# Skip weights folded into a scan's kernels, and the input turns of the scan moved in front of the first attention logits

## The chip, the cores and the metric

The program runs on one core of a Trainium2 chip. A core has a matrix engine (PE, with its weight loads PEld), a vector engine (VectorE, DVE in the rows), a scalar engine (ScalarE, ACT), GpSimd (POOL) and SyncE (SP), which here only issues DMAs. The metric is the device time of one execution in microseconds (us), the median of several runs. Matrix sums go to PSUM banks of 512 fp32 columns, which VectorE and ScalarE empty.

## The reference, cut to what matters

The program is a chain of transformer blocks; only one branch of the first and its neighbour are touched. `u` is 512 columns of the first projection, in 32 groups of 16 channels:

```python
uf = u.reshape(bsz, L, SSM_GROUPS, SSM_GROUP)           # 1024 tokens, 32 groups of 16
bu = einsum('gnp,blgp->blgn', B, uf)                    # complex, 64 states a group
s  = associative_scan(decay, bu)
y  = (einsum('gpn,blgn->blgp', C_re, s_r) - einsum('gpn,blgn->blgp', C_im, s_i)
      + D_skip.reshape(SSM_GROUPS, SSM_GROUP) * uf)
y  = gelu(y.reshape(bsz, L, SSM_WIDTH))
y  = y * sigmoid(y @ w_glu + b_glu)
```

Beside it stands sparse attention: for each of 8 heads and 8 blocks of 128 queries, logits against the keys up to the block, a mask of the 256 best keys (found earlier), softmax, and the product with the values. `D_skip` is the skip weight: each channel's input is added to its output, times one number.

## The kernel before, in words

Three stages matter, one after the other, each ended by all engines.

**`first_projection`** computes the projection. SP issues its loads and stores; between the second weight load and the first store it issues 12 small loads of gains (`HeadRows.load_gains`, L537).

**`sparse_prepare`** (about 180 to 215 us) turns queries and keys and, in between, makes the scan's weights. In `scan_group`, PE makes for every odd group four *kernels* of the scan: `K` (16 input channels by 128 = 8 time steps times 16 output channels) is the sum of two products of 64 states (L2026). `K` goes to memory and comes back later as a block of a Toeplitz matrix. There are eight such groups of four. Per block of 128 rows PE does eight turns (L2039), four turns of other weights (L2021), and the eight products of a `K` group. VectorE scales the next block's rows (L1993) before PE can turn them.

**`attend_and_scan`** (about 431 to 688 us) does attention and the scan together. Attention is a list of 64 *items*: pair of heads `n // 16`, block `n % 16 // 2`, head `n % 2`. Each item is: `logits(n)` on PE (L2600), `mask(n)` on VectorE (L2718), `exps(n)` on ScalarE (L2885), `turn(n)` on PE (L2610), `move(n)` on ScalarE (L2892), and every second item `values` on PE (L2619). `logits` runs two items ahead. Each engine's order is written out by one loop over `n`; the scan is threaded into it by the table `place`, which says at which item, and at which of two spots in it, a group of the scan's work is issued. The groups are eight each of:

- TURN_U: PE turns the regrouped inputs (L2628); ScalarE moves them to SBUF (L2915). Item 0 to 3.
- SUM_IN: PE multiplies them with the input weights (L2640); ScalarE moves (L2919). Items 4 to 7. After the last, VectorE and GpSimd run the scan itself in steps, one an item, from item 8 (`SCAN_AT`): L2738 on for VectorE, L2529 on for GpSimd.
- SUM_OUT: PE adds kernel part and state part (L2659, L2660); VectorE adds them to the inputs that were multiplied with the skip weights (L2804). Items 30 to 33, 35 and 36.
- Gelu on ScalarE at item 36 (L2953), then TURN_Y (L2667, moved in L2923), items 37 to 40, and MIX (L2678, L2930), items 41 to 48.

The skip multiplications are eight VectorE instructions of 128x512 (L2853), one an item at items 4 to 11. They wait only for GpSimd's regrouping (L2513).

Before the first logits the keys and the first queries are split in an upper and a lower part, in two halves of the columns: `upper_half` on ScalarE (L2876, L2869, L2871), `lower_half` on VectorE (L2822, L2825). The first half comes first of all, the second at item 0; it is needed for `logits(8)`. The TURN_U groups use three PSUM banks in turn, two of which are the second banks of the logits, which items 0 to 7 of a pair do not need.

## Time and profile before

| | us |
|---|---|
| median of three runs | 3916.5 |
| the three runs | 3909.71, 3976.51, 3916.5 |
| the profiled execution | 3910.52 |
| its span | 3908.8 |
| `sparse_prepare` in it | 180 to 215 |
| `attend_and_scan` in it | 431 to 688 |

The span is what the profiler saw of the instructions; the execution's own time has 1.7 us more around it. Times in rows count from the start of the span. PE is busy for 94% of the span, but that mean is over many stages; the two stages above are to be read from their own windows.

### The profile page before, as it was taken

To read this page: it belongs to the slowest core of one execution; us is meant where nothing else is said; L and a number is where in the kernel's file an instruction comes from. 1 tells how busy PE (TensorE), PEld (TensorE's weight loads), DVE (VectorE), ACT (ScalarE), POOL (GpSimd) and SP (SyncE) were. 2 spreads that over 40 slices of the span, in tenths; PEclk is the share of its full clock that TensorE was granted. 3 is DMA by queue.
4 is the path that set the end of the run, shared out by engine and by line. 5 is a ranking of instruction groups with operands and counts; after the bars stand their busy time and mean duration, and the time that the engine had idled before them with its cause. 6 is when DMAs were issued, how large, how long until landed. Compare 5 with 4: busy or idle time off the path is not lost. (4 is left out here: it accounts for less than half of the span.)

```text
span 3908.8 us, 53307 instructions
## 1 busy us (share of the span) xinstructions
PE 3665.5 (94%) x19688; PEld 3115.3 (80%) x19688; DVE 2537.2 (65%) x4296; ACT 1819.5 (47%) x3398; POOL 1219.0 (31%) x1199
## 2 busy tenths in 40 slices
PE   7999789898999999999999978899999999999898
PEld 6868666777888788788878877778899999999876
DVE  6679664346777576312675578876567777776666
ACT  3256466135333345321444457755445555545444
POOL 1423320141111101111235451100566666666400
PEclk9989999999999999999999989999999999999999
DMA  4322221562676574521235587855211111111064
GB/s 153 113 81 92 92 50 68 183 211 88 207 256 231 196 273 138 162 103 49 79 122 180 172 184 140 168 199 167 53 33 53 46 39 44 55 39 44 22 243 140
DMA packets 348750, 485.37 MB, mean 124 GB/s; under 512 B 45435, under 2 KB 219036, under 8 KB 344636
## 3 DMA queue, kind: packets, MB, share of 16 engines
q1 hardware_dynamic: 311580, 371.33, 30.2%
q0 software_dynamic: 34608, 106.45, 9.4%
q10 hardware_dynamic: 2304, 4.20, 0.3%
q8 instruction: 157, 2.57, 0.3%
q14 instruction: 101, 0.83, 0.1%
HBM read 337.43 MB, written 144.47 MB: 123 GB/s over the span
## 5 line engine op out<-in xcount | busy, mean ns | idle before, releaser
L119 PE MATMUL banks<-l_first_ws,l_XT 128*128 128x256 f32 x2880 | 359.6, 284 | 0.0
L119 PEld LDWEIGHTS banks<-l_first_ws,l_XT 128*128 128x128 f32 x2880 | 348.8, 192 | 0.0
L119 PE MATMUL banks<-l_XT,hg_ws 128*128 128x512 f32 x1440 | 343.2, 394 | 0.0
L119 PEld LDWEIGHTS banks<-l_XT,hg_ws 128*128 128x128 f32 x1440 | 266.7, 189 | 52.5
L4898 POOL TENSOR_TENSOR hg_DD<-hg_BB 128x256 f32<-128x256 f32 x224 | 173.9, 776 | 259.3 <-PE banks L4651 133.4
L4751 DVE TENSOR_TENSOR hg_DD<-hg_Q,hg_DD 128x256 f32<-128x256 f32 x224 | 204.7, 914 | 73.3 <-ACT hg_DD L4824 73.2
L119 PE MATMUL even_bank<-l_first_ws,l_XT 128*128 128x512 f32 x888 | 207.8, 392 | 3.2 <-PEq L909 1.9
L119 PE MATMUL even_bank<-even_ws,l_XT 128*128 128x512 f32 x876 | 204.4, 390 | 0.0
L119 PEld LDWEIGHTS even_bank<-l_first_ws,l_XT 128*128 128x128 f32 x888 | 167.3, 189 | 41.2 <-issue 6.0
L119 PEld LDWEIGHTS even_bank<-even_ws,l_XT 128*128 128x128 f32 x876 | 163.9, 188 | 34.0
L119 PE MATMUL am_g_acc<-l_XT,am_ws 128*128 128x512 f32 x768 | 176.1, 391 | 0.0
L4899 POOL TENSOR_TENSOR hg_DD<-hg_BB 128x256 f32<-128x256 f32 x224 | 170.2, 760 | 0.0
L119 PEld LDWEIGHTS am_g_acc<-l_XT,am_ws 128*128 128x128 f32 x768 | 144.2, 188 | 32.2 <-issue 0.8
L119 PE MATMUL down_acc<-down_first_split 128*128 128x512 f32 x696 | 162.7, 392 | 3.3 <-PEq L1496 3.3
L4751 DVE TENSOR_TENSOR hg_DD<-hg_KK,hg_DD 128x256 f32<-128x256 f32 x224 | 165.3, 738 | 0.0
L119 PEld LDWEIGHTS down_acc<-down_first_split 128*128 128x128 f32 x696 | 131.8, 189 | 31.2 <-issue 3.7
L4866 ACT ACTIVATE hg_junk<-banks 128x128 f32<-128x128 f32 x128 | 35.3, 276 | 227.1 <-DVE hg_O L4768 227.1
L4651 PE MATMUL banks<-hg_DD 128*128 128x128 f32 x896 | 121.8, 280 | 12.9 <-DVE hg_AT L4705 10.3
L3285 ACT ACTIVATE even_stage<-even_bank 128x512 f32<-128x512 f32 x48 | 28.7, 598 | 219.7 <-PE even_bank L119 219.7
L4651 PEld LDWEIGHTS banks<-hg_DD 128*128 128x128 f32 x896 | 115.8, 196 | 17.3 <-issue 6.9
L4824 ACT ACTIVATE hg_DD<-hg_DD 128x1024 f32<-128x1024 f32 x112 | 118.3, 1056 | 14.3 <-POOL hg_DD L4899 13.8
L119 PE MATMUL banks<-l_XT 128*128 128x512 f32 x504 | 121.0, 399 | 2.5 <-PEq L4562 1.9
(771 smaller groups left out, 9213.8 us busy)
## 6 DMA issues: line engine op xcount, KB each, us to landing
l_first_raw<-in_odd_w_in SPq DMA_DIRECT2D x64, 512.0 KB, 5.5
l_first_raw<-in_even_w_in SPq DMA_DIRECT2D x16, 1024.0 KB, 5.4
l_room_tiles<-hidden SPq DMA_DIRECT2D x63, 256.0 KB, 6.9
da_first_X<-q_k_hi POOLq DMA_DIRECT2D x24, 512.0 KB, 8.0
da_first_X<-q_k_lo POOLq DMA_DIRECT2D x24, 512.0 KB, 13.1
l_room_tiles<-y_even SPq DMA_DIRECT2D x45, 256.0 KB, 5.7
ffn_y<-in_w_ffn_down SPq DMA_DIRECT2D x22, 512.0 KB, 4.5
weight_sums_w_ffn_down<-ffn_y SPq DMA_DIRECT2D x11, 1024.0 KB, 4.2
```

Source lines behind the costliest of these rows:

```text
L119: mm = pe.matmul(out, lhs(p, k), rhs(q, k), start=start and i == 0, stop=stop and i == n - 1, skip_group_check=skip)
L3285: act.activation(stage[:, i % B, :], bank[:, i % B, :], chunks[i // G][2]).then_inc(moved, 1)
L4651: mm = pe.matmul(pA[:, u % 2, i * P:(i + 1) * P], DD[:, buf(n, l), 0, i, :], DD[:, buf(n, l), 1, i, :], start=True, stop=True, skip_group_ ...
L4751: last = dve.tensor_tensor(d, sides(x[:, s, :], h)[:, :, e, :, u, :], d, ALU.mult)
L4824: act.activation(d, d, ACT.Exp).then_inc(es, 1)
L4866: act.activation(junk[:, j % 2, :], pO[:, j % 2, 0:R_D], ACT.Square, accum_out=hs[:, sb, 0, j:j + 1]).then_inc(sqd, 1)
L4898: pool.tensor_tensor(factors(n, j, 1)[:, :, :, 1 - e, :], b[:, :, :, 1 - e, :], mid, ALU.subtract)
L4899: last = pool.tensor_tensor(factors(n, j, 0)[:, :, :, e, :], mid, b[:, :, :, e, :], ALU.subtract)
```

## The change

Four things are changed, all in the stages above.

1. The skip weights go into the kernels `K`. They are loaded early, as 16 x 32 numbers; VectorE makes from them 32 diagonal blocks of 16 x 16 (`through`), and in `scan_group` PE adds one to the first 16 columns of each kernel, by a product with the identity between the two that were there. The eight skip multiplications are gone, the later addition of outputs to inputs becomes a copy, and the skip load in front of the stage too.
2. TURN_U 0 to 2 are issued in front of the first logits, 3 to 6 at item 0, 7 at item 1. VectorE moves them, not ScalarE.
3. The second half of keys and queries is split at item 3, not 0. The exp table is loaded after the first casts, not before.
4. All later scan work is issued earlier: SUM_IN by one item, the scan's steps by one, SUM_OUT and all behind it by two. SUM_IN 4 and 5 and TURN_Y 3 and 4 use other banks.

```diff
@@ HeadRows
+        self.skip_w = place.sb("skip", [S_CH, S_GROUPS], side="right")
     def load_gains(self, sp):
+        sp.dma_start(self.skip_w[:, :], self.skip.rearrange("(g q) -> q g", q=S_CH),
+                     allow_slow_non_contiguous=True).then_inc(self.skip_ld, DMA)
         sp.wait_ge(self.ones, 1)
@@ sparse_prepare, VectorE, then PE
+                dve.wait_ge(head.skip_ld, DMA)
+                dve.tensor_tensor(through[:, :, :], ident[0:S_CH, 0:S_CH].unsqueeze(1).to_broadcast([S_CH, S_GROUPS, S_CH]),
+                                  head.skip_w[:, :].unsqueeze(2).to_broadcast([S_CH, S_GROUPS, S_CH]), ALU.mult).then_inc(diagonal, 1)
                 mean_of(0)
...
+                    if i == 1:
+                        pe.wait_ge(diagonal, 1)
...
-                        for c in range(2):
-                            mm = pe.matmul(acc[0:S_CH, b, q * P:(q + 1) * P], ss.cB[rows, c, j, :], ss.CP[rows, c, j, 0:S_T, :],
-                                           start=c == 0, stop=c == 1)
+                        pe.matmul(out, ss.cB[rows, 0, j, :], ss.CP[rows, 0, j, 0:S_T, :], start=True, stop=False)
+                        pe.matmul(out[:, 0:S_CH], ident[0:S_CH, 0:S_CH], through[:, 2 * j + n % 2, :], start=False, stop=False,
+                                  skip_group_check=True)
+                        mm = pe.matmul(out, ss.cB[rows, 1, j, :], ss.CP[rows, 1, j, 0:S_T, :], start=False, stop=True)
@@ attend_and_scan, the table of places
-        place[k // 2, k % 2] = TURN_U + k
-        place[4 + k // 2, k % 2] = SUM_IN + k
-        place[(30 + k, 1) if k < 4 else (35 + (k - 4) // 2, k % 2)] = SUM_OUT + k
-        place[37 + k // 2, k % 2] = TURN_Y + k
-        place[41 + k, 1] = MIX + k
+        place.setdefault(((-1, 0), (-1, 0), (-1, 0), (0, 0), (0, 0), (0, 1), (0, 1), (1, 0))[k], []).append(TURN_U + k)
+        place[3 + k // 2, k % 2] = [SUM_IN + k]
+        place[(28 + k, 1) if k < 4 else (33 + (k - 4) // 2, k % 2)] = [SUM_OUT + k]
+        place[35 + k // 2, k % 2] = [TURN_Y + k]
+        place[39 + k, 1] = [MIX + k]
-    bank_no.update({SUM_IN + k: (8 + k) % 3 if k < 4 else 0 for k in range(8)})
+    bank_no.update({SUM_IN + k: (8 + k) % 3 if k < 6 else 0 for k in range(8)})
-    bank_no.update({TURN_Y + k: (1, 2, 0, 0, 0, 0, 0, 0)[k] for k in range(8)})
+    bank_no.update({TURN_Y + k: (1, 2, 0, 1, 2, 0, 0, 0)[k] for k in range(8)})
-    SKIP_AT, HALVE_AT, SCAN_AT, GELU_AT, MULT_AT = 4, 10, 8, 36, 49
+    LATER_AT, HALVE_AT, SCAN_AT, GELU_AT, MULT_AT = 3, 10, 7, 34, 47
@@ VectorE
-                    dve.tensor_tensor(yv, bank_at(SUM_OUT + k).rearrange("c g (s q) -> c g s q", q=S_CH), yv, ALU.add).then_inc(out_add, 1)
+                    dve.tensor_copy(yv, bank_at(SUM_OUT + k).rearrange("c g (s q) -> c g s q", q=S_CH)).then_inc(out_add, 1)
+                        if TURN_U <= g < SUM_IN:
+                            k = g - TURN_U
+                            dve.wait_ge(u_made, k + 1)
+                            dve.tensor_copy(U[:, 4 * k:4 * k + 4, :], bank_at(g)).then_inc(u_moved, 1)
-                    if n == 0:
+                    if n == LATER_AT:
                         lower_half(1)
-                    if SKIP_AT <= n < SKIP_AT + S_T:
-                        s = n - SKIP_AT
...
-                        dve.tensor_tensor(uc[:, s, :], uc[:, s, :], skip_w, ALU.mult).then_inc(skipped, 1)
@@ ScalarE
+                upper_half(0)
                 act.preload_act_table_set(LOG_EXP)
-                upper_half(0)
-                    if n == 0:
+                    if n == LATER_AT:
                         upper_half(1)
```

VectorE's order at the start of `attend_and_scan`, before. L2822 and L2825 are the lower parts of keys and queries; L2718 (ISA) is a mask, with its row minimum as a row of its own.

```order
L2822 TENSOR_TENSOR aa_K<-merge_first_F,aa_K 128x512
L2825 TENSOR_TENSOR aa_X<-merge_first_F,aa_X 64x512 x2
L2718 ISA aa_S,aa_least<-aa_pS,att_M 128x128
L2718 ISA aa_least 128x1
L2718 ISA aa_S,aa_least<-aa_pS,att_M 128x128
L2718 ISA aa_least 128x1
L2822 TENSOR_TENSOR aa_K<-merge_first_F,aa_K 128x512
L2825 TENSOR_TENSOR aa_X<-merge_first_F,aa_X 64x512 x2
L2718 ISA aa_S,aa_least<-aa_pS,att_M 128x256
```

The same place now. L2832 is VectorE's move of a TURN_U group (line numbers differ between the kernels).

```order
L2832 COPY aa_three<-aa_acc 128x512
L2832 COPY aa_three<-aa_pS 128x512 x2
L2839 TENSOR_TENSOR aa_K<-merge_first_F,aa_K 128x512
L2842 TENSOR_TENSOR aa_X<-merge_first_F,aa_X 64x512 x2
L2731 ISA aa_S,aa_least<-aa_pS,att_M 128x128
L2731 ISA aa_least 128x1
L2731 ISA aa_S,aa_least<-aa_pS,att_M 128x128
L2731 ISA aa_least 128x1
L2832 COPY aa_three<-aa_acc 128x512
L2832 COPY aa_three<-aa_pS 128x512 x2
L2832 COPY aa_three<-aa_acc 128x512
L2731 ISA aa_S,aa_least<-aa_pS,att_M 128x256
```

Three copies now stand ahead of the first split, and four between the second mask and the third, where the second split stood.

ScalarE's order at items 3 and 4 now. L2897 is an exp, L2904 a move of turned exps, L2930 a move of a SUM_IN group, L2914 and L2915 empty a bank of values, L2888 to L2883 are the upper parts of the second half.

```order
L2897 ACTIVATE aa_E<-aa_S,aa_least 128x384
L2930 ACTIVATE aa_three<-aa_pS 128x4x128
L2904 ACTIVATE aa_ET<-aa_pE 128x2x128
L2914 ACTIVATE aa_part<-aa_pO 64x128
L2915 ACTIVATE aa_yo<-aa_pO 64x128
L2914 ACTIVATE aa_part<-aa_pO 64x128
L2915 ACTIVATE aa_yo<-aa_pO 64x128
L2930 ACTIVATE aa_three<-aa_acc 128x4x128
L2888 ACTIVATE aa_K<-merge_first_F 128x512
L2881 ACTIVATE aa_X<-merge_first_F 64x512
L2883 ACTIVATE aa_X<-merge_first_F 64x512 x2
L2897 ACTIVATE aa_E<-aa_S,aa_least 128x384
```

The second half's casts now stand between the exps of items 4 and 5, behind two SUM_IN moves and the first emptying of values; before, they stood at item 0, behind two TURN_U moves.

## Rows read from the trace of the kernel before

**Rows 1.** The page: the span, and busy time of each engine with its share.

```profile
span 3908.8 us, 53307 instructions
PE 3665.5 (94%) x19688; PEld 3115.3 (80%) x19688; DVE 2537.2 (65%) x4296; ACT 1819.5 (47%) x3398; POOL 1219.0 (31%) x1199
```

**Rows 2.** Windows: stretch, length; busy of PE, PEld, DVE, ACT, POOL; clock; DMA share, GB/s.

```profile
437.00:453.00 16.00, 11.97 (x54) 10.51 (x54) 6.28 (x19) 10.87 (x25) 0.45 (x1) 0.69 0.76 199
453.00:470.00 17.00, 16.69 (x173) 13.40 (x174) 5.02 (x13) 12.24 (x28) 0.04 (x1) 1.00 0.01 2
470.00:500.00 30.00, 19.55 (x90) 16.11 (x89) 29.65 (x32) 16.55 (x30) 19.67 (x10) 0.83 0.02 9
500.00:530.00 30.00, 24.18 (x118) 18.69 (x117) 28.76 (x37) 19.56 (x50) 11.82 (x5) 0.94 0.03 10
575.00:600.00 25.00, 17.01 (x88) 14.52 (x89) 7.52 (x16) 21.49 (x34) 0.00 (x0) 0.80 0.12 42
```

**Rows 3.** Timeline, 431 to 446: start, busy, engine, line, operation, [idle before <- releaser].

```profile
431.08 1.28 ACT L2933 ACT_TABLE_LOAD   x1 [0.57 <-PEq L2132]
431.26 4.44 POOL L2513 COPY aa_three<-att_scan_inputs 128x1024 f32<-128x1024 f32 x4 [7.04 <-POOLq L2132]
434.83 2.13 DVE L2825 TENSOR_TENSOR aa_X<-merge_first_F,aa_X 64x512 fp32r<-64x512 f32 x2 [1.01 <-ACT aa_X L2871]
437.11 1.85 PE L2600 MATMUL aa_pS<-aa_K,aa_X 128*128 128x128 f32 x6 [8.16 <-DVE aa_X L2825]
438.75 1.06 PE L2628 MATMUL aa_acc<-ident,aa_three 128*128 128x128 f32 x4
439.85 0.60 ACT L2915 ACTIVATE aa_three<-aa_acc 128x512 f32<-128x512 f32 x1 [0.88 <-PE aa_acc L2628]
445.78 0.62 PE L2600 MATMUL aa_pS<-aa_K,aa_X 128*128 128x384 f32 x2 [2.56 <-DVE aa_least L2718]
```

**Rows 4.** Timeline, 453 to 472: the SUM_IN groups and the scan's first step.

```profile
456.39 1.09 PE L2640 MATMUL aa_pS<-aa_three 128*64 128x128 f32 x16
464.42 0.82 DVE L2718 CUSTOM_DVE_ANT_0 aa_S<-aa_pS,att_M 128x640 f32<-128x640 f32 x1 [2.21 <-PE aa_pS L2600]
465.33 1.56 PE L2619 MATMUL aa_pO<-aa_ET,att_V 128*128 128x256 f32 x6
469.77 1.23 DVE L2738 TENSOR_TENSOR merge_first_F<-aa_three,aa_s_wide 128x1024 f32<-128x1024 f32 x1 [3.71 <-ACT aa_three L2919]
```

**Rows 5.** The skip multiplications: all eight by line, then the timeline, 471 to 487.

```profile
L2853 DVE TENSOR_TENSOR att_scan_inputs<-att_scan_inputs,merge_first_F x8: 684/687/2844, 449.7 to 489.1; 128x512 f32<-128x512 f32 x8
...
471.79 2.00 DVE L2853 TENSOR_TENSOR att_scan_inputs<-att_scan_inputs,merge_first_F 128x512 f32<-128x512 f32 x1
479.38 2.36 POOL L2535 TENSOR_TENSOR merge_first_F<-aa_three,aa_s_wide 128x1024 f32<-128x1024 f32 x1
479.45 2.84 DVE L2853 TENSOR_TENSOR att_scan_inputs<-att_scan_inputs,merge_first_F 128x512 f32<-128x512 f32 x1
482.32 4.51 DVE L2830 TENSOR_TENSOR aa_X<-merge_first_F,aa_X 64x1024 fp32r<-64x1024 f32 x2
```

**Rows 6.** DMA issues, 530 to 566 us: line, count, KB each, us to landing.

```profile
aa_s_wide<-scan_out SPq DMA_DIRECT2D x8, 256.0 KB, 5.4
```

**Rows 7.** Timeline, 577 to 583: PE waits for a bank behind ScalarE's Gelu work.

```profile
581.74 1.51 PE L2600 MATMUL aa_pS<-aa_K,aa_X 128*128 128x512 f32 x4 [4.45 <-ACT aa_three L2923]
```

**Rows 8.** Timeline, one period of `sparse_prepare`, then the nearest small products.

```profile
194.13 1.64 PEld L2026 LDWEIGHTS ap_acc<-l0s_s_wide,l0s_s_cB 64*16 64x16 f32 x16 [0.17 <-issue]
195.98 0.86 PEld L2039 LDWEIGHTS ap_pT<-ident,ap_xs 128*128 128x128 f32 x8 [0.21 <-DVE ap_xs L1993]
...
1654.33 0.66 PE L3155 MATMUL even_bank<-ident,even_t 16*128 16x16 f32 x8
```

**Rows 9.** SP's timeline, 39 to 48: the gains' loads, and the first store.

```profile
39.13 5.09 SPq L537 DMA_DIRECT2D l0s_gc<-in_q_norm_g  x8
47.75 11.56 SPq L604 DMA_DIRECT2D first_projection<-l0s_stage  x3
```

More of the change, by code:

```diff
@@ L517, with __init__ @@
     EARLY, WIDTH = 4, 964
-    def __init__(self, place, gains):
-        self.gains, self.place = gains, place
+    def __init__(self, place, gains, skip):
+        self.gains, self.place, self.skip = gains, place, skip
         self.raw = place.sb("first_raw", [P, KD, NC], side="right")
@@ L523, in __init__ @@
         self.gain = place.sb("gc", [P, 8], side="right")
+        self.skip_w = place.sb("skip", [S_CH, S_GROUPS], side="right")
+        self.skip_ld = place.sem("skip_loaded")
         flat = self.raw[:, :, :].rearrange("p k n -> p (k n)")
@@ L1871, in sparse_prepare @@
         stage = pl.sb("stage", [P, B, NC])
+        through = pl.sb("through", [S_CH, S_GROUPS, S_CH])
         pT = pl.ps("pT", [P, 2, 8, P])
@@ L2341, in __init__ @@
         self.uc = self.room[:, :].rearrange("c (s f) -> c s f", s=S_T)
-        self.skip, self.m8, self.bias = F[:, 7, 0:S_W], F[:, 7, S_W:S_W + S_J], F[:, 7, S_W + S_J:S_W + S_J + 4]
-        self.uc_ld, self.m8_ld, self.skip_ld, self.bias_ld = (
-            place.sem(n) for n in ("inputs_loaded", "radius_loaded", "skip_loaded", "mix_bias_loaded"))
+        self.m8, self.bias = F[:, 7, 0:S_J], F[:, 7, S_J:S_J + 4]
+        self.uc_ld, self.m8_ld, self.bias_ld = (place.sem(n) for n in ("inputs_loaded", "radius_loaded", "mix_bias_loaded"))
         self.loads = [(self.uc, p1[:, 0:S_W].rearrange("(c s) f -> c s f", s=S_T), self.uc_ld),
                       (self.m8, kept["m8"], self.m8_ld),
-                      (self.skip, prm["D_skip"].partition_broadcast(P), self.skip_ld),
                       (self.bias, prm["b_glu"].rearrange("(k p) -> p k", p=P), self.bias_ld)]
@@ L2407, in attend_and_scan @@
         t1, t2, p1t, p2t, p3t = (F[:, r, :].rearrange("p (j c) -> p j c", c=S_C) for r in (5, 6, 4, 0, 1))
-        skip_w, m8, bias = begun.skip, begun.m8, begun.bias
-        uc_ld, m8_ld, skip_ld, bias_ld = begun.uc_ld, begun.m8_ld, begun.skip_ld, begun.bias_ld
+        m8, bias, uc_ld, m8_ld, bias_ld = begun.m8, begun.bias, begun.uc_ld, begun.m8_ld, begun.bias_ld
         sum_banks = [acc[:, :, :]] + [pS[:, a, 1, :].rearrange("p (q n) -> p q n", n=P) for a in range(2)]
@@ L2682, in scan_part, with scan_group @@
                 def scan_part(n, spot):
-                    g = place.get((n, spot), -1)
+                    for g in place.get((n, spot), ()):
+                        scan_group(g)
+                def scan_group(g):
                     if TURN_U <= g < SUM_IN:
@@ L2693, in scan_part @@
                         mix_outputs(g - MIX)
+                scan_part(-1, 0)
                 pe.wait_ge(k_split, 1)
@@ L2814, in scan_part @@
                 def scan_part(n, spot):
-                    g = place.get((n, spot), -1)
-                    if SUM_OUT <= g < TURN_Y:
-                        add_output(g - SUM_OUT)
+                    for g in place.get((n, spot), ()):
+                        if TURN_U <= g < SUM_IN:
+                            k = g - TURN_U
+                            dve.wait_ge(u_made, k + 1)
+                            dve.tensor_copy(U[:, 4 * k:4 * k + 4, :], bank_at(g)).then_inc(u_moved, 1)
+                        elif SUM_OUT <= g < TURN_Y:
+                            add_output(g - SUM_OUT)
                 def lower_half(half):
@@ L2833, in _ @@
                 steps = scan_states()
+                scan_part(-1, 0)
                 lower_half(0)
@@ L2910, in scan_part, with scan_group @@
                 def scan_part(n, spot):
-                    g = place.get((n, spot), -1)
-                    if TURN_U <= g < SUM_IN:
-                        k = g - TURN_U
-                        act.wait_ge(u_made, k + 1)
-                        act.activation(U[:, 4 * k:4 * k + 4, :], bank_at(g), ACT.Copy).then_inc(u_moved, 1)
-                    elif SUM_IN <= g < SUM_OUT:
+                    for g in place.get((n, spot), ()):
+                        scan_group(g)
+                def scan_group(g):
+                    if SUM_IN <= g < SUM_OUT:
                         k = g - SUM_IN
@@ L4966, in build_program @@
             late = Place(nc, "l0s").__enter__()
-            head = HeadRows(late, (a["q_norm_g"][0], a["k_norm_g"][0], a["idx_k_norm_g"][0]))
+            head = HeadRows(late, (a["q_norm_g"][0], a["k_norm_g"][0], a["idx_k_norm_g"][0]), a["D_skip"][0])
             with Place(nc, "l0w") as pw:
```

10 lines of the change are left out of this document (4 added, 6 removed).

## The prediction

> **What bounds the kernel now.** The page's shares [rows 1] say that PE is busy for 94% of the span, but the change touches two stages of some 290 us, so I read windows of them first [rows 2], then the timeline where PE has gaps. In `attend_and_scan` the bound changes place. From 437 to 453 PE is busy for 11.97 of 16 us at a granted clock of 0.69, a mixture of both levels (1.2 and 2.4 GHz); it then runs full until the last SUM_IN group (16.69 of 17 us at 1.00). From 470 to 500 VectorE is the bound (29.65 of 30 us, PE 19.55), and still from 500 to 530 (28.76, PE 24.18): attention's masks stand in one queue with the scan's steps. From 575 to 600 it is ScalarE (21.49 of 25, PE 17.01), with Gelu and the moves behind it. Outside these, PE is. A microsecond taken from VectorE is worth one only between 470 and about 535.
>
> The start, by its timeline [rows 3]: ScalarE loads a table for 1.28 us, casts, and VectorE splits; the first logits start at 437.11, 8.16 us after PE's last work. TURN_U groups follow, 1.06 us for four turns at the low level, each moved by ScalarE in 0.60. The splits of the second half hold VectorE, and PE waits 2.56 us for a mask. The scan's first step starts at 469.77, 3.71 us after VectorE's last work [rows 4], waiting for the last SUM_IN move.
>
> **The change, part by part.** Sums are made against the profiled execution's own time, 3910.5 us.
>
> *The start.* The table load no longer precedes the casts: 1.28 us earlier. In front of the first split VectorE now copies three groups. Regrouping takes GpSimd 4.44 / 4 = 1.11 us a quarter [rows 3], so its second quarter, which the third group needs, is there at 433.5. Three groups of turns behind it end at about 435 (one of 1.06 us after 433.5, plus a second's rest), the copy at 435.7. A copy of this shape out of PSUM isn't in the rows on VectorE; ScalarE's takes 0.60, an element-wise one on VectorE 0.69 [rows 5]; I take 0.65. Then the splits (0.1 to 0.8 us for the keys and 2.13 for the queries; with GpSimd's copies over, some 2.3 together): first logits at 438.0, **0.9 us later**, with three groups done.
>
> *From there to the scan's first step.* PE was busy for 11.97 + 16.69 = 28.7 us from 437 to 470 [rows 2]. Off go three groups of 1.06 (3.2) and one item's attention work, since SUM_IN ends at item 6: the values there alone are 1.56 us [rows 4], with a logits and a turn I take 3. That leaves 22.5. Onto it come new waits, which follow from the order. The mask of item 5 stands behind the second split, and that behind ScalarE's queue of item 3: two SUM_IN moves (1.2), the emptying of a bank (about 1.1, four short instructions), the casts (2.5, the distance from the table load's end to the first query split in [rows 3]), then 2.1 for the split. That is 7 us of standstill on VectorE, with only some 5 us of PE work ready in it (four SUM_IN groups of 1.09 and a logits [rows 4]): about 2.4 us of waiting. `logits(8)` now waits for the bank of SUM_IN 5, moved by the ScalarE that is late: 2. The last SUM_IN waits for the one before it in the same bank: 0.9. Sum 22.5 + 5.3 + 0.6 for the last move = 28.4; the first step starts at 466.4, 3.4 us earlier. But it is item 7's step: the mask of item 9 (0.82 [rows 4]) and little else of attention now lies behind it. **Worth 3.4 - 0.8 = 2.6 us.** Who waits on the standstill: the exps of item 5 and with them PE's turns.
>
> *The skip multiplications.* Eight go. Five are over before 470, in VectorE's idle time: nothing. Three lie in its bound stretch: 2.00, 2.84, and 0.69 (the median and the last) [rows 5]; 5.5 us as recorded, 2.1 of undisturbed work. The 2.84 begins 0.07 us behind a GpSimd step of 2.36 us that also has two SBUF inputs, and it takes as long as the two together. What stands behind it also has two (L2830, 4.51 us for two) and would take that wait over. Bounds 2.1 and 5.5; I take **3.4**, because one of the two disturbed multiplications is followed by such an operation that is itself already delayed, and the other's wait may go.
>
> The Trainium skill, page "SBUF — State Buffer", section "SBUF: two separate sides", calls the port pair of VectorE and GpSimd "an exclusive lock, not a bandwidth split", for VectorE operations with two SBUF inputs against GpSimd ones that read SBUF. The 2.84 and 2.36 fit it. By that rule the wait belongs to GpSimd's steps and not to the multiplication, so the sum would hold 2.1 here; that is a rival below. It speaks for the copies out of PSUM too, which have one input there.
>
> *Additions into copies.* 0.69 to about 0.65, eight times, while PE is the bound: 0.
>
> *Two items earlier.* SUM_OUT, Gelu, TURN_Y and MIX keep their work. SUM_OUT 4 needs the last load of output weights, issued once the second states are ready: 5.4 us to land [rows 6], plus 2.6 of issue. Between lie three items instead of four; with the long values of item 31 I count about 8 us of PE work there, so a new wait of 0 to 2 us is possible, with the values of item 33 queued behind. `logits(40)` now shares a bank with TURN_Y 3, two items back, where it waited 4.45 us for TURN_Y 0 [rows 7]. But ScalarE bounds that stretch, so most of this wait comes back as one for exps, and PE has smaller items to cover it. Bounds -4.5 and +3; I take **1 us gained**.
>
> *`sparse_prepare`.* Eight groups get four small products each. The 16 records for eight products [rows 8] make two of one: 8 records more a group. The nearest small ones are eight records in 0.59 us from the first's start to the next instruction's (busy 0.66) [rows 8]. PE waited only 0.21 us a period for VectorE, so 0.4 comes through, in the five of seven periods without a larger wait: **2.0 us lost**. Bounds 0 (all under waits) and 8 x 0.6 = 4.7. The diagonals are one VectorE operation of 512 columns before anything else, where it would wait for ScalarE's squares: 0; without this cover 0.7.
>
> *The skip load.* Now 512 single numbers in one DMA, issued by SP in front of the gains. The nearest row is 64 single numbers: 5.09 / 8 = 0.64 us of issue [rows 9]. Between 0.64 and eight times that, 5.1 us, the gains and the first store, issued at 47.75, shift. Four stage buffers stand behind the store, and `sparse_prepare`, the first user, starts at 180: 0. If the cover were short, up to 4 us once.
>
> The Trainium skill, "DMA: Bandwidth & Descriptors", section "Rules for kernel authors", says that a non-contiguous last dimension is lowered to one descriptor per element and should be rearranged. It speaks against this load; no row here shows its landing. By it the load would be slow, but its user comes 140 us later, so the sum stays.
>
> **Sum**: -2.6 - 3.4 - 1.0 + 2.0 = -5.0 us, own time 3905.5. The median before is 6.0 above the profiled execution and the lowest run 0.8 below; the mean of the two close runs is 3913.1. I forecast 3913.1 - 5 = **3908 us**.
>
> **Rivals.**
>
> 1. *The wait moves on* (chance 0.22). Each GpSimd step delays one VectorE step, whichever; 2.1 for 3.4, and the wait for banks comes back whole: -2.6 - 2.1 + 2, and 1 us of wait in front of SUM_OUT 4: -1.7, 3911. For it: L2830 is slow with no multiplication in between. Against: nothing much.
> 2. *Slower: the split at item 3* (0.17). If PE stays at the low level through its waits, as [rows 3] show at the start, the four SUM_IN groups before the standstill's end and the turns take double, some 6 us, and ScalarE's queue shifts alike. The first step then starts at 472.5, +2.7 + 0.8; with 2.1 saved and 2.5 lost in `sparse_prepare`, +3.9: 3917. It decides once the first step starts later than about 471.4 (469.8 + 1.6, where my sum is zero). Against: PE starts four us sooner, before the clock has fallen.
> 3. *All comes through* (0.13): 5.5 for the multiplications, 4.45 for the bank, no loss in `sparse_prepare`: -2.6 - 5.5 - 4.5 = -12.6: 3900.
> 4. *Small products cost what large ones do* (0.04): 64 records of 0.10 us (1.64 / 16 [rows 8]), all coming through: +6.6 for +2, 3913, with nothing gained in that half.
>
> Forecast (-2 to -8 us) 0.44.
>
> **Range and chances.** The unknown costs reach from -12.6 to +6 us, 3900 to 3919. Three runs lay 7 us apart even without the highest, which adds to both ends. 3894 to 3922 leaves out less than 2 in 10. A measurement of this kernel tells from no change about 2%, 78 us; no case comes near. Within 2%: 0.98, 0.01 on each side.
>
> **What would show it.** Right: first logits at 438 and the scan's first step near 466; no 2.56 us wait for the third mask, but VectorE idle for some 5 to 7 us before the sixth; three 128x512 operations fewer between 470 and 495; `sparse_prepare` longer by 2 us; the stage's end earlier by 5 to 7 relative to its start. Wrong: a first step after 471; the GpSimd delay on other operations at its full sum; PE idle in front of SUM_OUT 4; or a `sparse_prepare` period above 3.7 us.

## The result, and the profile after

The changed kernel took 3923.9 us in the median of 14 runs (3917.2 to 3929.6), the kernel before 3910.8 in as many beside it; the ratio is 1.0033, 95% interval [1.0026, 1.0040]. It is 13 us slower, by far less than the 2% that count as a change, but beyond the top of the forecast range (3922), and on the other side of the kernel before than the forecast (3908). The profiled execution took 3925.7 us. Three executions lie far above the others of their kernels (3976.5 and 9335.5 us of the kernel before, 8160.7 us of run 2 below) and are left out of the ratios.

The page of the changed kernel, span and busy time, answers to [rows 1]:

```profile
span 3923.9 us, 53426 instructions
...
PE 3679.9 (94%) x19752; PEld 3116.6 (79%) x19752; DVE 2537.8 (65%) x4297; ACT 1817.9 (46%) x3390; POOL 1217.7 (31%) x1199
```

PE is busy for 14.4 us more, with 64 records more; the other engines are as before. Where these lie is found by stages. I compare when each begins, in both traces: `sparse_prepare`'s first turn (179.9 us before, 179.0 after), the next stage's first product (215.5 and 225.1), GpSimd's first regrouping in `attend_and_scan` (431.3 and 443.1), ScalarE's first operation of the stage behind it (690.2 and 702.0). So `sparse_prepare` takes 46.1 us instead of 35.6, the stage behind it, untouched, 218.0 instead of 215.8, and `attend_and_scan` 258.9 in both: it neither gains nor loses. At the stage borders behind it, up to 2320 us, the distance is 11.6 to 11.9 us; some 3 us more come later, in untouched stages.

Windows of the changed kernel, columns as in [rows 2]; the first lies in `sparse_prepare`, the others are those of [rows 2] moved by 11.8 us:

```profile
190.00:200.00 10.00, 10.00 (x51) 5.99 (x51) 3.04 (x9) 3.71 (x11) 0.80 (x3) 0.50 0.30 110
448.80:464.80 16.00, 14.27 (x109) 11.77 (x109) 6.95 (x19) 8.00 (x19) 0.04 (x1) 0.79 0.82 200
464.80:481.80 17.00, 14.14 (x110) 11.22 (x111) 7.90 (x15) 11.16 (x25) 4.19 (x2) 0.90 0.00 1
481.80:511.80 30.00, 19.61 (x98) 16.22 (x98) 29.04 (x31) 18.76 (x34) 16.22 (x9) 0.89 0.03 10
511.80:541.80 30.00, 22.61 (x111) 17.42 (x110) 29.28 (x38) 20.12 (x49) 10.97 (x6) 0.94 0.03 10
586.80:611.80 25.00, 19.08 (x73) 14.62 (x74) 5.64 (x12) 19.07 (x34) 0.00 (x0) 0.73 0.01 2
```

In `sparse_prepare` PE is recorded as busy without a gap, at a granted clock of 0.50, the low level, with VectorE and ScalarE at a third: PE has become the bound there, and it gets only 51 matmuls done in 10 us. The same 10 us before, with 81 of them:

```profile
190.00:200.00 10.00, 9.36 (x81) 7.48 (x79) 7.01 (x21) 7.10 (x27) 2.38 (x9) 1.00 0.52 183
```

In `attend_and_scan` VectorE is still the bound from 481.8 on (29.04, then 29.28 of 30).

The stage's start, by its timeline (columns as in [rows 3]), answers to [rows 3] and [rows 4]:

```profile
444.19 0.66 PE L2637 MATMUL aa_acc<-ident,aa_three 128*128 128x128 f32 x4 [3.40 <-POOL aa_three L2522]
444.88 0.69 DVE L2832 COPY aa_three<-aa_acc 128x512 f32<-128x512 f32 x1 [3.15 <-PE aa_acc L2637]
445.38 1.28 ACT L2945 ACT_TABLE_LOAD   x1
449.21 1.85 PE L2609 MATMUL aa_pS<-aa_K,aa_X 128*128 128x128 f32 x6 [3.03 <-DVE aa_X L2842]
...
462.19 0.69 DVE L2839 TENSOR_TENSOR aa_K<-merge_first_F,aa_K 128x512 fp32r<-128x512 f32 x1 [4.81 <-ACT aa_K L2888]
463.99 1.40 DVE L2842 TENSOR_TENSOR aa_X<-merge_first_F,aa_X 64x512 fp32r<-64x512 f32 x2 [1.10 <-ACT aa_X L2883]
466.05 1.22 PE L2609 MATMUL aa_pS<-aa_K,aa_X 128*128 128x512 f32 x2 [2.38 <-DVE aa_least L2731]
473.05 0.87 PE L2609 MATMUL aa_pS<-aa_K,aa_X 128*128 128x512 f32 x4 [1.42 <-ACT aa_three L2930]
477.41 1.22 DVE L2751 TENSOR_TENSOR merge_first_F<-aa_three,aa_s_wide 128x1024 f32<-128x1024 f32 x1 [2.62 <-ACT aa_three L2930]
```

Counted from GpSimd's first regrouping (443.10; 431.26 before), the first logits stand at 6.1 us (5.9 before), the scan's first step at 34.3 (38.5 before; 35.1 forecast).

### The profile page after: what moved, and what is told of

Same layout as the page of the kernel before. It is cut to its first block and busy times, and to the rows that moved or that the text cites. A ratio compares the mean times of both kernels' runs of the same rounds, so it can differ in the third digit from the quotient of the medians.

```text
span 3923.9 us, 53426 instructions
## 1 busy us (share of the span) xinstructions
PE 3679.9 (94%) x19752; PEld 3116.6 (79%) x19752; DVE 2537.8 (65%) x4297; ACT 1817.9 (46%) x3390; POOL 1217.7 (31%) x1199
## 5 line engine op out<-in xcount | busy, mean ns | idle before, releaser
L4909 POOL TENSOR_TENSOR hg_DD<-hg_BB 128x256 f32<-128x256 f32 x224 | 174.7, 780 | 258.9 <-PE banks L4662 133.0
L4662 PEld LDWEIGHTS banks<-hg_DD 128*128 128x128 f32 x896 | 115.0, 195 | 17.2 <-issue 6.9
L4835 ACT ACTIVATE hg_DD<-hg_DD 128x1024 f32<-128x1024 f32 x112 | 118.4, 1057 | 14.4 <-POOL hg_DD L4910 13.9
```

The lines of the kernel that those rows point to most:

```text
L4662: mm = pe.matmul(pA[:, u % 2, i * P:(i + 1) * P], DD[:, buf(n, l), 0, i, :], DD[:, buf(n, l), 1, i, :], start=True, stop=True, skip_group_ ...
L4835: act.activation(d, d, ACT.Exp).then_inc(es, 1)
L4909: pool.tensor_tensor(factors(n, j, 1)[:, :, :, 1 - e, :], b[:, :, :, 1 - e, :], mid, ALU.subtract)
```

## Experiments

Times are medians; each ratio is to the kernel before on the same chip. Besides, each trace gives the lengths of the stages, cut as above. They repeat more closely than the time of the whole, and most verdicts rest on them; there is one trace for each run. "Low level" is the part of `sparse_prepare` in which the granted clock was 0.50, added up from windows of 1 us. "16 rows" are the small products as the change has them.

```
small products   run                  sparse_prepare  low level  next stage  attend_and_scan
none             before                    35.6         10.2       215.8         258.9
16 rows          changed                   46.1         23.9       218.0         258.9
none             1                         35.1         13.7       214.1         264.4
16 rows, twice   3                         43.7         13.6       218.1         258.5
none             4                         35.2         10.4       219.0         259.8
64 rows          5                         35.5         10.2       217.8         256.5
16 rows          6                         39.1          7.3       219.0         259.1
none             7                         35.9         10.2       219.1         259.2
none             8                         35.5         13.7       214.1         259.5
64 rows          9                         37.5         13.7       216.5         260.3
none             10                        35.5         13.7       214.3         260.2
none             11                        35.9         10.2       214.2         256.5
none             12                        35.8         11.2       219.0         258.7
16 rows          13, changed again         46.2         23.9       217.9         258.7
16 rows          14, changed again         39.1          7.3       219.0         259.0
16 rows          15, as 6                  46.1         23.9       218.0         259.2
16 rows          16, as 6                  52.0         37.6       219.1         259.6
```

### The small products

**1. Without them.**

```diff
-                        pe.matmul(out[:, 0:S_CH], ident[0:S_CH, 0:S_CH], through[:, 2 * j + n % 2, :], start=False, stop=False,
-                                  skip_group_check=True)
```

> The changed kernel without the 32 small products of `sparse_prepare`; the load of the skip weights and the VectorE operation that makes the diagonals stay. The skip term is thus left out of the result. Theory A (the products themselves made the stage long, each like a large one, and kept TensorE at the low level): the stage from its first work to the next stage's first product is as long as before (some 38 us instead of 48), its period of a tile at full clock falls from 4.27 to 3.31 us, the 2.2 us at the start of the next stage go too, and the time is 3923.9 - 12.7 = 3911 us. Rival B (the load of single numbers or the diagonal operation holds up the stage's start, the products cost 2 us as forecast): 3922 us, and the first squares stay late. In `attend_and_scan` both expect the same as in the changed kernel: 0 net against the kernel before.

3915.8 us, ratio 1.0016 [1.0006, 1.0025]: 8 us below the changed kernel, not 13. The stage is 35.1 us long, with the load and the diagonals in place. Rival B has fallen. But 5 us above the kernel before are left, clear of zero, where theory A had 3911; they are taken up under runs 9 and 10.

**2. One product of 64 columns for a group of four.**

```diff
+                        pe.matmul(acc[0:S_CH, b, :].rearrange("c (q m) -> c q m", m=P)[:, :, 0:S_CH], ident[0:S_CH, 0:S_CH],
+                                  through[:, g:g + 7:2, :], start=False, stop=False, skip_group_check=True)
```

> The changed kernel with one small product for a group of four instead of four: stationary the same 16x16 identity, moving 64 columns, output the four 16-column pieces of the bank; the four first large products come ahead of it, the four second ones behind. Theory A1 (the cost is by the instruction: a 16-column product takes what a 128-column one takes): a quarter of the cost is left, period 3.31 + 0.24 = 3.6 us, stage 2 to 3 us longer than before, time 3914. Rival A2 (the cost is that of interrupting two accumulating products, or of a low clock once begun): the order changes in every group of four, so the stage stays within 2 us of the changed kernel's 48 us, 3922 to 3924.

3914.4 us in the median of eleven, ratio 1.0013 [1.0003, 1.0023]. One product instead of four takes most of the cost away, which speaks for A1 (3914) against A2 (3922 to 3924). It doesn't tell whether it is the product or the change to it that costs, since both went from four to one. Its one trace is that of the execution of 8161 us, so nothing is read from it.

**3. Each small product twice.**

> The changed kernel with each small product issued twice (the skip term is counted twice in the result). Theory A: another 4 x 0.23 = 0.9 us a group at full clock, 1.6 at the low one, so 8 to 13 us more in the stage: 3932 to 3937. Rival B (the products are mostly hidden and something else costs the stage): within 2 us of 3923.9.

3925.5 us, ratio 1.0036 [1.0023, 1.0049]: 1.5 above the changed kernel, and the stage no longer than its 46.1. Theory A missed by far. Rival B's time came true, but its cause had fallen with run 1. The timeline shows why A missed. First the changed kernel, PE and its weight loads, around one small product at full clock:

```profile
206.61 0.39 PE L2037 MATMUL ap_acc<-l0s_s_wide,l0s_s_cB 64*16 64x128 f32 x2
206.93 0.11 PEld L2038 LDWEIGHTS ap_acc<-ap_through,ident 16*16 16x16 f32 x2 [0.21 <-issue]
206.93 0.21 PE L2038 MATMUL ap_acc<-ap_through,ident 16*16 16x16 f32 x2
207.07 0.39 PE L2040 MATMUL ap_acc<-l0s_s_wide,l0s_s_cB 64*16 64x128 f32 x2
207.30 0.38 PE L2037 MATMUL ap_acc<-l0s_s_wide,l0s_s_cB 64*16 64x128 f32 x2
```

The same place with two small products (L2038, L2040):

```profile
214.14 0.11 PEld L2038 LDWEIGHTS ap_acc<-ap_through,ident 16*16 16x16 f32 x2 [0.21 <-issue]
214.15 0.21 PE L2038 MATMUL ap_acc<-ap_through,ident 16*16 16x16 f32 x2
214.19 0.11 PEld L2040 LDWEIGHTS ap_acc<-ap_through,ident 16*16 16x16 f32 x2
214.21 0.20 PE L2040 MATMUL ap_acc<-ap_through,ident 16*16 16x16 f32 x2
214.34 0.39 PE L2042 MATMUL ap_acc<-l0s_s_wide,l0s_s_cB 64*16 64x128 f32 x2
```

The second starts 0.06 us behind the first and lengthens a tile's period from 4.27 to 4.47 us, 0.05 for each. The first lengthens it from 3.31 to 4.27, 0.24 for each, and its weight load stands idle for 0.21 us, though nothing is waited for. (In the records 64\*16 is a weight of 64 rows and 16 columns.) What costs is not the product but getting to it.

**5. The same product on 64 rows.**

```diff
-                        pe.matmul(out[:, 0:S_CH], ident[0:S_CH, 0:S_CH], through[:, 2 * j + n % 2, :], start=False, stop=False,
-                                  skip_group_check=True)
+                        pe.matmul(out[:, 0:S_CH], ident[rows, rows.start:rows.start + S_CH], through[rows, 2 * j + n % 2, :],
+                                  start=False, stop=False, skip_group_check=True)
```

> The changed kernel with each small product on 64 rows instead of 16, the same 64 rows as the large products around it: stationary a 64x16 piece of the identity, moving the diagonals padded with zeros. Number, place and columns of the products stay, so does the result. The third experiment's second product cost 0.05 us, the first one 0.24, with 0.21 us between them in which the weight load stands. Theory S (that 0.19 is the price of going from weights of 64 rows to weights of 16): the period falls from 4.27 to 3.31 + 4 x 0.05 to 0.07 = 3.5 to 3.6 us, the stage is 2 us longer than without the products, time 3918. Rival T (it is the price of any new accumulating product between two others, or of its 16 columns): period still 4.2 to 4.3, time 3924.

```profile
206.40 0.38 PE L2042 MATMUL ap_acc<-l0s_s_wide,l0s_s_cB 64*16 64x128 f32 x2
206.62 0.20 PE L2043 MATMUL ap_acc<-ap_through,ident 64*16 64x16 f32 x2
206.67 0.38 PE L2045 MATMUL ap_acc<-l0s_s_wide,l0s_s_cB 64*16 64x128 f32 x2
```

The next large product starts 0.05 us behind the small one, no weight load stands idle there, and the period is 3.51 us, as theory S has it. Of the 0.24 us a product, 0.19 was the change from weights of 64 rows to weights of 16 and back. The Trainium skill, page "TensorEngine Tiling (Array Packing)", section "Key Properties", says that changing the tiling mode drains TensorE, and its list of modes has tiles of 64 and of 32 rows. That 16 rows fall into another mode than 64 is my reading of that list; the idle weight load of 0.21 us fits it.

This edit changes the number of rows and, in every second group, also which rows: there the large products stand on rows 64 to 127, and the small one of the changed kernel on rows 0 to 15. In the other groups both begin at row 0. The changed kernel's period is the same 4.27 us behind either kind of group (six times in a row in run 14), so it is the number of rows and not their place.

The stage is 35.5 us, as long as without products; 3919.6 us, ratio 1.0019 [1.0010, 1.0029]. The time doesn't follow the stage: it is 9 us above the kernel before, and run 9 with the same products 7. Why is not shown.

**6. The products alone, on the kernel before.** (`sparse_prepare` and the load as changed, `attend_and_scan` as before.)

> The kernel before with only the changes in `sparse_prepare`: the load of the skip weights ahead of the gains, the diagonals, the 32 small products; `attend_and_scan` as before, so the skip term is counted twice in the result. Theory A (the products are the whole loss): 3911 + 8 to 10 = 3920 us, the stage some 44 to 46 us to the next stage's first product, `attend_and_scan` as before. Rival E (part of the loss comes from the moved work of `attend_and_scan`): nearer to 3916.

3923.5 us, ratio 1.0029 [1.0016, 1.0041], from eight executions between 3914.4 and 3929.8: as much as the whole change, without any of the other edits. Yet its trace has a stage of 39.1 us, not the 44 to 46 that A asked for. Hence the last four runs.

**13 to 16. The stage again, twice in the changed kernel and twice as in 6.**

> The changed kernel once more, for the length of `sparse_prepare` (first turn to the next stage's first product; 46.1 us in its first trace) and of the low level in it. If the low level comes with the products, 44 to 46 us again; if by chance, anything from 39 (the sixth experiment) to 46. The period at full clock is 4.27 us in either case.

> The changed kernel a third time, with the same two expectations: 44 to 46 us of the stage if the low level comes with the products, anything from 39 to 46 if by chance.

> The sixth experiment once more (the skip term is counted twice). If the low level comes with the products: 44 to 46 us instead of its 39.1. If by chance: between 39 and 46. The lengths of the next stage (219.0 us, before 215.8) and of the one behind `attend_and_scan` (201.8, before 198.2) tell whether those, too, were chance: then one of them near the lower value.

> The sixth experiment a third time, with the same two expectations as the run ahead of it: 44 to 46 us of `sparse_prepare` if the low level comes with the products, 39 to 46 if by chance.

46.2, 39.1, 46.1 and 52.0 us, in single runs of 3928.5, 3918.0, 3927.4 and 3933.7 us. The same 10 us as in the changed kernel's first window, in run 14 and then in run 16:

```profile
190.00:200.00 10.00, 10.00 (x86) 6.37 (x84) 6.92 (x20) 6.57 (x22) 1.60 (x6) 1.00 0.52 181
```

```profile
190.00:200.00 10.00, 10.00 (x51) 5.95 (x51) 3.04 (x9) 3.70 (x11) 0.79 (x3) 0.50 0.33 120
```

PE has no recorded gap in either; one gets 86 matmuls done, the other 51. The instructions of the stage are the same in all six traces, so nothing in them sets how long the low level lasts (7.3 to 37.6 us); for this document it is chance. Each microsecond of it costs 0.42 to 0.43: (46.1 - 39.1) / (23.9 - 7.3), (52.0 - 39.1) / (37.6 - 7.3). Without products 10 to 14 us of low level leave the stage at 35 to 36, since there PE has slack behind VectorE. With 10.2 us of low level, in the kernel before, it waits twice:

```profile
184.72 1.97 PE L2039 MATMUL ap_pT<-ident,ap_xs 128*128 128x128 f32 x8 [0.91 <-DVE ap_xs L1993]
201.06 1.82 PE L2039 MATMUL ap_pT<-ident,ap_xs 128*128 128x128 f32 x8 [1.70 <-DVE ap_xs L1993]
```

With 13.7 us, in run 1, only 0.27 us of waiting is left; with the products there is none even in run 14. The shortest stage with products fits this: 8 groups at 0.96 are 7.7 us, less 2.6 for those two waits and 1.2 for 2.9 fewer microseconds of low level, an estimate of 3.9 against 3.5 measured. The mean of the six traces with these products is 44.8 us, **9.2 us** above before: 3.5 with the fewest low microseconds, and 5.7 from the rest. That more of it falls on kernels with these products is seen in four traces of six, and not explained.

### The start, the multiplications, the places

**4. Without products, outputs two items later.**

```diff
-    LATER_AT, HALVE_AT, SCAN_AT, GELU_AT, MULT_AT = 3, 10, 7, 34, 47
+    LATER_AT, HALVE_AT, SCAN_AT, GELU_AT, MULT_AT = 3, 10, 7, 36, 49
```

and SUM_OUT, TURN_Y, MIX and TURN_Y's banks as before.

> The kernel of the first experiment (no small products, skip term left out) with SUM_OUT, Gelu, TURN_Y and MIX put back two items later, and the banks of TURN_Y as before; the start of `attend_and_scan` stays as changed. Theory C (the early places give back the 2.7 us that the start had gained: exps of items 30 and 31 wait for masks, TensorE's wait for Gelu falls among larger items, and the clock stays low longer): 2 to 3 us less than the first experiment, 3908.5, and the masks from item 43 on at their old distance less 2.7 us. Rival D (the gain of the start is lost at any place, because the scan's work ends no earlier against the loads of the output weights): within 0.7 us of the first experiment, 3911.

3911.4 us, ratio 1.0002 [0.9993, 1.0011], 4.4 below run 1, as theory C asks. With the items where they were, the masks can be followed one by one against the kernel before, counted from the stage's start: item 14 is 2.2 us early, item 29 still 2.4, most from item 33 on 1.0, the last 0.9. So the time goes against D, but the masks go against C: the 2.7 us don't come back with the late places.

**8. Only the multiplications gone** (GpSimd adds the weights in `sparse_prepare`, as in 7).

> The kernel before with the eight skip multiplications gone from `attend_and_scan` and the weights added by GpSimd in `sparse_prepare`; turns, splits, places and banks as before. The result is the reference's. By my forecast's term the multiplications are worth 3.4 us (bounds 2.1 and 5.5) where VectorE is the bound: the masks from item 19 on come 2 to 5 us earlier in the stage, time 3907.5. Rival (the wait passes to the operations behind them, and what is left is given back at the outputs): masks 2 us earlier at item 19, nothing at the end, 3911.

3911.1 us, ratio 1.0004 [0.9994, 1.0013]. Masks 18 to 29 are 1.5 us early, less than the lower bound of 2.1, and from item 32 on none is early: the rival, and less than that. VectorE's timeline of this kernel shows who took the waits over (both splits of the next queries in one row; 4.51 us before [rows 5]):

```profile
474.93 6.57 DVE L2856 TENSOR_TENSOR aa_X<-merge_first_F,aa_X 64x1024 fp32r<-64x1024 f32 x2
481.53 3.25 DVE L2768 TENSOR_TENSOR aa_three<-merge_first_F 128x1024 f32<-128x1024 f32 x1
```

In the changed kernel it is, among others, an operation of four columns that stands through a step of GpSimd. Before, it took 0.16 us, and the multiplication behind it 2.84 [rows 5]. The row of before, then two of the changed kernel:

```profile
479.38 0.16 DVE L2847 TENSOR_SCALAR merge_first_F<-merge_first_F 128x4 f32<-128x4 f32 x1
```

```profile
489.86 2.40 POOL L2546 TENSOR_TENSOR merge_first_F<-aa_three,aa_s_wide 128x1024 f32<-128x1024 f32 x1
489.97 2.31 DVE L2865 TENSOR_SCALAR merge_first_F<-merge_first_F 128x4 f32<-128x4 f32 x1
```

What eats the rest lies at 96 to 110 us of the stage. PE waits 2.8 to 2.9 us there for a move in all of these kernels. Windows of 14 us over that place, of the kernel before, then of run 8, then of run 7:

```profile
527.30:541.30 14.00, 11.05 (x65) 9.30 (x64) 13.17 (x19) 13.13 (x24) 2.38 (x2) 1.00 0.27 52
```

```profile
524.70:538.70 14.00, 11.04 (x55) 9.13 (x54) 12.80 (x19) 11.54 (x21) 2.38 (x2) 0.88 0.42 75
```

```profile
530.60:544.60 14.00, 11.15 (x54) 9.10 (x53) 13.13 (x18) 11.52 (x21) 2.39 (x2) 0.88 0.90 128
```

In the same busy time PE does 65 matmuls before and 55 or 54 with the masks earlier. The clock is 1.00 in the four traces whose `attend_and_scan` is as before (before, 6, 15, 16), and falls in twelve of the other thirteen traces (in run 1 a little later; run 5 is the exception). A clock of 0.88 over 14 us is 3.4 us at the low level, and half of that, 1.7, is the work lost by it; the masks lose 1.4 to 1.6 us between items 29 and 33 in runs 4, 7, 8, 11 and 12. That the clock is the cause is argued from these sizes, and no run holds it fixed. Why it falls at this place only when the masks are earlier stays open.

**7, 11 and 12. GpSimd adds the weights, outputs late, split at item 3, 2, 0.**

```diff
+                    y = stage[0:S_CH, b, :].rearrange("p (g m) -> p g m", m=P)[:, :, 0:S_CH]
+                    pool.tensor_tensor(y, y, through[:, g:g + 7:2, :], ALU.add).then_inc(added, 1)
```

with SP's store of the group waiting for `added`, no small products, and LATER_AT 3, 2, 0.

> The changed kernel's start of `attend_and_scan`, no small products, SUM_OUT and what follows two items later as before, and the skip weights added to the kernels by GpSimd instead (eight additions of 16x64 numbers into the stored tiles, while GpSimd has nothing else). The result is the reference's. Theory (the additions are hidden, the start gives 2.7 us and loses 1.4 to 1.8 again to a low-level stretch in front of the outputs): 0 to 1 us below the kernel before, 3910. Rival (the additions hold up ScalarE's stage buffers and so `sparse_prepare`): 2 us or more above the fourth experiment.

> The seventh experiment with the second half of the keys split at the third item instead of the fourth. Theory (in the changed kernel TensorE stands for some 5.7 us around item 6 since the mask of item 5 is behind this split; an item earlier it has SUM_IN groups left to fill it): the scan's first step up to 1 us earlier in the stage than the 34.1 us of the seventh, the time within 1 us of it. Rival: the split's wait for ScalarE only moves, the first step stays at 34 us.

> The seventh experiment with that split back after the first item, the turns still in front of the first logits and moved by VectorE. It takes the split's part out of the start's gain. Theory (the gain comes from the turns alone): first step at 34 us of the stage, and the masks of items 5 to 10 not late. Rival (the later split is what gave it): first step at 37 to 38.5 us, as before. Of the time, 3911 to 3914 either way.

3914.4, 3910.0 and 3914.7 us; ratios 1.0004 [0.9994, 1.0013], 0.9998 [0.9989, 1.0007], 1.0006 [0.9997, 1.0015]. An addition of run 7 takes 0.31 us on GpSimd, and `sparse_prepare` is as long as before, in all three. So run 7's 3.0 us above run 4 are what its rival asks for, but don't come from where the rival says; both kernels' executions spread over 11 to 14 us. The addition, behind its wait for ScalarE's move:

```profile
195.73 0.31 POOL L1932 TENSOR_TENSOR ap_stage<-ap_stage,ap_through 16x64 f32<-16x64 f32 x1 [4.55 <-ACT ap_stage L1973]
```

The scan's first step stands at 34.1, 33.0 and 35.3 us of the stage (38.5 before). So the turns in front give 3.2 of the gain and the place of the split 1.2, though run 12's masks of items 5 to 10 are 0.9 to 3.3 us late all the same. One item earlier would have given 1.1 more: run 11's masks are 4.3 us early at item 29, and still 2.5 at the end, the best of the series. Its total is not told from the kernel before.

**9 and 10. The places once more.** 9 is run 5 with late outputs, 10 is run 7 with early ones.

> The fifth experiment (small products on 64 rows, result the reference's) with SUM_OUT, Gelu, TURN_Y and MIX two items later, as before. Theory L (the early places cost some 3 us in the median, as 3915.8 against 3911.4 between the first and the fourth experiment): 3919.6 - 3 = 3916.5 us. Rival M (that difference was spread; the places are worth nothing either way): 3919 us.

> The seventh experiment (GpSimd adds the skip weights, result the reference's) with the early places of the changed kernel. Theory L: 3914.4 + 3 = 3917.5 us. Rival M: 3914 us. Both expect `sparse_prepare` as long as before, 35.5 to 36 us to the next stage's first product.

3918.2 and 3918.8 us; ratios 1.0018 [1.0010, 1.0027], 1.0013 [1.0004, 1.0023]. The early places are slower in all three pairs (4.4, 4.4 and 1.4 us in the medians; 4.8, 2.4 and 1.9 in the means), but each kernel has 11 or 12 runs spread over 11 to 17 us. The three pairs together tell what none of them does alone: the mean of their differences is 3.0 us, and drawing the runs of each kernel anew puts 95% of it between 1.0 and 5.0. That speaks for theory L.

The length of the stage hardly shows it: its mean is 259.5 us in the seven traces with early places and no other edit in the stage (changed, 13, 14, 3, 5, 1, 10), and 259.8 in the three with late ones and the same split (4, 7, 9). One difference is in the rows, though. In six of those seven traces PE waits in front of SUM_OUT for a load of output weights (0.17 us in the changed kernel, 0.29, 0.30, 0.57, 0.82, and 2.7 in run 1), and in none of the ten with the places of before. Run 1:

```profile
536.72 0.46 PE L2666 MATMUL aa_acc<-aa_MTa,aa_three 128*128 128x128 f32 x2 [1.86 <-DMA aa_s_wide<-scan_out]
558.22 0.46 PE L2666 MATMUL aa_acc<-aa_three 128*128 128x128 f32 x2 [0.83 <-DMA aa_s_wide<-scan_out]
```

These are half of the 5.5 us by which run 1's stage is longer than before. How often so long a wait comes in the executions without a trace, and so whether it is the 3 us, is not shown.

## Why the forecast was wrong

**The step that failed first is the cost of the small products in `sparse_prepare`: +2.0 us forecast, +9.2 measured.** I priced a small product from eight records that follow each other with one shape [rows 8], 0.59 us for eight. That is right for the products alone: 0.05 us each, 0.2 us a tile (runs 3 and 5). But there they stand between products of 64 rows, and each pays 0.19 us to change over. The row to take was in the same group: [rows 8] has the weight load waiting 0.17 and 0.21 us where the shape changes from turns to 64\*16 and back, and I read one as a wait for VectorE. In the changed kernel, where PE is late and VectorE long done, the same change still shows it:

```profile
209.42 0.86 PEld L2052 LDWEIGHTS ap_pT<-ident,ap_xs 128*128 128x128 f32 x8 [0.21 <-issue]
```

So there was no such wait to hide a part of the cost. At four times a group it is 0.96 us a group, 7.7 in all, instead of the 0.6 and 4.7 that I took as the upper bound. Of that, 3.5 us came through in the two traces (runs 6 and 14) with the least of the low level. The other 5.7 of the mean are a term that I did not have: with the last waits gone from the stage, each microsecond at the low level costs 0.42. My sign "a period above 3.7 us" came: 4.27. Rival 4 was nearer for this term (+6.6, from 64 records at 0.10), from a wrong cause; its time, 3913, was still 11 us short, and 0.04 was too little for it.

**The second step that failed is the gain in `attend_and_scan`: -7.0 us forecast (2.6 + 3.4 + 1.0), 0 in the stage.** It is as large a part of the miss as the first. The next four paragraphs take its terms one by one.

**The start: right, and better than forecast.** First logits 0.3 us later in the stage instead of 0.9; VectorE idle for 4.81 + 1.10 us at the split (5 to 7 forecast); PE waiting 2.38 us for the mask behind it (2.4) and 1.42 for the bank of SUM_IN 5 (2); first step 4.2 us earlier instead of 3.4. Rival 2 did not come.

**The multiplications: -3.4 forecast, -1.5 until item 29, 0 at the end** (run 8). Rival 1 named the mechanism, a wait that moves to whatever VectorE does next. The page of the Trainium skill that goes with it, "SBUF — State Buffer", section "SBUF: two separate sides", names a 2-port mode of VectorE beside two SBUF inputs as a ground for the lock. The 2.31 us for four columns, with one input, fit that if the operation ran in such a mode, which no row shows.

**The places: -1.0 forecast, nothing gained in the stage, and by runs 1, 4, 5, 7, 9 and 10 some 3 us lost in the time.** SUM_OUT waits 0.2 us for a load in the changed kernel's first trace, but 2.7 in run 1 with the same places: the new wait of 0 to 2 us that the forecast allowed for does come. The wait for the bank came back almost in full. In the changed kernel PE stands behind the same ScalarE work [rows 7], now for a move:

```profile
590.03 0.87 PE L2619 MATMUL aa_pE<-ident,aa_E 128*128 128x128 f32 x3 [4.20 <-ACT aa_ET L2904]
```

**What became of the stage's gain.** 2.65 us at item 29 (changed kernel), of 6.0 forecast for the start and the multiplications. What was left seems to have gone in the clock: from 96 to 180 us of the stage PE is idle for 12.1 us instead of 13.9, but at the low level for 17.2 us instead of 10.2 (windows of 2 us). In runs 3 and 13, whose `attend_and_scan` has the same instructions, the last mask is still 2.0 to 2.2 us early, but the stage is only 0.2 to 0.4 shorter; there the low level comes later, 7 us of it behind 180 us instead of 4. This is argued from the traces; no run isolates it. I ended VectorE's bound stretch at about 535 us and counted what was gained in it as gained.

**The load and the diagonals: 0, right.** SP's timeline and the load's own row answer to [rows 9]:

```profile
40.05 0.57 SPq L535 DMA_DIRECT2D l0s_skip<-in_D_skip  x1
40.66 5.12 SPq L541 DMA_DIRECT2D l0s_gc<-in_q_norm_g  x8
...
48.38 0.58 SPq L608 DMA_DIRECT2D first_projection<-l0s_stage  x1
```

```profile
l0s_skip<-in_D_skip SPq DMA_DIRECT2D x1, 2.0 KB, 8.0
```

It is issued at the price of a load of 64 numbers, the lower bound, and lands 8.0 us later, 131 us ahead of its user. A load of 1808 KB, issued 0.4 us before it, takes 8.2:

```profile
l0s_first_raw<-in_w_in SPq DMA_DIRECT2D x1, 1808.0 KB, 8.2
```

So it lands as late as that load, which may have stood in its way. The rule that the prediction cites from the Trainium skill, "DMA: Bandwidth & Descriptors", section "Rules for kernel authors" (one descriptor per element), would make it slow too; no run here tells the two apart.

**The sum with the measured terms.** The forecast started from 3913.1 us; the kernel before turned out at 3910.8 in fourteen runs, which hid 2.3 us of the miss by luck. With the terms above it is 3910.8 + 9.2 + 0 = 3920.0 us, against a median of 3923.9. The miss of 16 us is 7.2 of `sparse_prepare`, 7.0 of the gain that didn't come, and 3.9 that are left, less those 2.3. The 3.0 us of the early places would nearly close it, but run 6, which has none of them, stands at 3923.5 too. So the last 4 us stay open; the untouched stage behind `sparse_prepare` alone takes from 214.1 to 219.1 us in 17 traces.

## What to carry to other kernels

Price an inserted instruction by its neighbours, not only by its own kind: a row of like instructions hides what it costs to change over to them and back, and a small matmul of another row height than those around it cost five times its own work here. Padded with zeros to their height, it cost only its own 0.05 us there, though the two kernels made so are still 7 to 9 us above the kernel before. And a microsecond won where one engine is the bound has to be followed to the stage's end before it goes into the sum: none of 2.7 arrived in the changed kernel, 2.5 of 4.3 in run 11.

## What was not expected of the hardware

- TensorE with weights of 16 rows between weights of 64: 0.24 us a product, 0.21 of it with the weight load idle; with 64 rows 0.05.
- The low level under records without a gap: 51 matmuls in 10 us at 0.50, 86 at 1.00 in another run of the same kernel. It lasted from 7.3 to 37.6 us of the stage. Two executions of the changed kernel with 7.3 and 23.9 us of it took 3918.0 and 3928.5 us.
- A VectorE operation of four columns took 2.31 us beside a GpSimd step of 2.40, and 0.16 before.
